# Expert products in plain float32: three groups of 32 slots in four column groups of TensorE, in place of split products over 128 slots

## The chip, the cores and the metric

One core of a Trainium2 chip runs the kernel. The metric is the device time of one launch in microseconds, lower is better. The core has a matrix engine (TensorE, PE in the rows; PEld is its weight load), three engines for elementwise work (VectorE or DVE, ScalarE or ACT, GpSimd or POOL), and SyncE (SP), which here starts nearly all DMA transfers. Sixteen DMA engines move the data between HBM and the on-chip memory. Products land in PSUM, eight banks of 128 partitions x 512 float32.

## What is computed

Two decoder layers over 256 tokens of width 1024. The change touches the last part of the second layer: eight experts, of which each token takes two.

```python
def swiglu(h, w_gate, w_up, w_down):
    return (jax.nn.silu(h @ w_gate) * (h @ w_up)) @ w_down

def moe_swiglu(h, w_router, w_gate, w_up, w_down):
    ...
    logits = (t @ w_router).astype(F32)
    top_v, top_i = lax.top_k(logits, TOP_K)
    wts = jax.nn.softmax(top_v, axis=-1)
    gate = jnp.sum(jax.nn.one_hot(top_i, N_EXPERTS, dtype=F32) * wts[..., None], axis=1)
    out = jnp.zeros((bsz * L, D), F32)
    for e in range(N_EXPERTS):
        ye = swiglu(t, w_gate[e], w_up[e], w_down[e]).astype(F32)
        out = out + gate[:, e:e + 1] * ye
```

D_MODEL is 1024, D_FF_EXPERT 3584, N_EXPERTS 8, TOP_K 2. All is float32: the experts' weights are 8 x 3 x 1024 x 3584 values, 352 MB, and each is read once.

## The kernel before

The kernel is written for each engine on its own, with semaphores between them. Both mixers and the dense channel mixer of layer one come first; `experts()` (one function for each engine, at L1290 for TensorE, L2004 for ScalarE, L2778 for VectorE) is the rest.

**Routing.** VectorE ranks the router's logits and gives each token a slot in each of its experts (`slot_of`). An expert has 128 slots. TensorE gathers the tokens of the first two experts by a product with a one-hot matrix (`gather`, L1481); for the others GpSimd fetches normalised rows from HBM by an indirect DMA (`taken`), and TensorE transposes them (`taken_transposes`, L1400). The outputs of experts 0 to 6 are scaled and added to rows in HBM by an indirect DMA of GpSimd (`sums`); those of expert 7 are combined on TensorE by another one-hot product.

**Split products.** A float32 product is made of three products of a rounded type (float32r). ScalarE rounds a weight tile to `hi` (L1910), VectorE subtracts to get `lo` (L2628), and `split_product` (L819 to L821) multiplies activation high by weight high, high by low and low by high. In each of them the activations are the stationary operand, 128 rows x 128 slots, and the weights are the moving one, 512 columns. `hi` and `lo` have three buffers each, so both engines run at most three tiles ahead of TensorE.

**Tiles and order.** A tile holds 2048 columns on 128 partitions, 1 MB: four blocks of 128 rows x 512 columns of a gate or up matrix, or 256 rows x 1024 of a down matrix. An expert takes 42 tiles in seven steps of 512 hidden columns: two gate, two up and two down tiles a step, with TensorE on the down tiles of one step behind the hidden ones of the next. Each tile costs TensorE 12 matmuls. SP loads them into a ring of seven places (`ring_e` and, for the seventh, `hT`); a place is free again when VectorE has made its `lo`. Between the steps ScalarE applies SiLU (L2074), VectorE multiplies (`act_product`, L2640), TensorE transposes the result (L1354) and both engines split it again (L2079, L2633).

**More than 128 tokens for one expert.** A second pass over all weights then runs; it is under an `If` on `most`, the largest count of tokens.

Of the kernel before, what the change touches and what calls it, by code (L numbers as in the profile page):

```python
# [20 lines left out]
P = 128  # L21
# [11 lines left out]
def decoder_trunk(nc, x_in, mem_in, positions, norm_mix, w_in, a_re, a_im, log_dt, b_re, b_im,  # L33
# [42 lines left out]
    MOE_TILES = 6 * NFE  # L76
    assert COLS == IN_FULL * BANK + 256 and FF % 256 == 0 and FE % BANK == 0 and NF % 2 == 1
# [13 lines left out]
    with ctx:  # L91
# [19 lines left out]
        normed = renamed("normed", [P, C, D], F32)  # L111
        xT_hi = sb("xT_hi", [P, KD, SEQ], F32R)
# [29 lines left out]
        memT = sb("memT", [P, KD, MEM])  # L142
        mask = sb("mask", [P, NG * 3 * P])
# [16 lines left out]
        last_ring.close()  # L160
        gT_hi = renamed("gT_hi", [P, KS, SEQ], F32R)
# [54 lines left out]
        fb = buffers(ffn)  # L216
        hi = fb("hi", [P, H, TILE], F32R)
# [20 lines left out]
        fb("idle", [P, (KD - 3) * P - 128])  # L238
# [3 lines left out]
        y_hi = fb("y_hi", [P, D], F32R)  # L242
        y_lo = fb("y_lo", [P, D], F32R)
# [11 lines left out]
        most = fb("most", [P, 1], I32)  # L255
        ffn.close()
# [13 lines left out]
        def combines_before(e):  # L270

            return e - (NE - 1)

# [167 lines left out]
        full_e = [sem(f"expert_tile_arrived_{r}") for r in range(RM)]  # L441
        params = sem("params_loaded")
        lrates = [sem(f"layer_rates_loaded{l}") for l in range(L)]
        lparams = [sem(f"layer_params_loaded{l}") for l in range(L)]
        N_SMALL = 7
        BASE = [0, MIX_TILES + FFN_TILES]

# [6 lines left out]
        def load_rates(queue, l):  # L454

            rates = lrates[l]
# [4 lines left out]
        def load_matrices(queue, l):  # L461

            s = lparams[l]
# [9 lines left out]
        def _(sp):  # L473
# [62 lines left out]
            def load_e(p, e, src, first):  # L536

                if not first or p >= RM:
                    sp.wait_ge(sem("lo_ready"), FFN_TILES + MOE_TILES * e + p - RM + 1)
                elif p == RM - 1:  # L540
                    sp.wait_ge(sem("logits_done"), 1)
                v = expert_tile(p).rearrange("p (k n) -> p k n", n=src.shape[2])
                sp.dma_start(v, src).then_inc(full_e[p % RM], 16)
# [12 lines left out]
            def expert_loads(e, turn, first):  # L556
                for i in range(4):
                    load_e(i, turn, moe_src(e, 0, i), first)
                for f in range(1, NFE):
                    for i in range(4):  # L560
                        load_e(6 * f - 2 + i, turn, moe_src(e, f, i), first)
                    for i in range(2):
                        load_e(6 * f + 2 + i, turn, moe_down_src(e, f - 1, i), first)
# [2439 lines left out]
```

## Time and profile before

| | |
|---|---|
| median of 3 runs | 1742.5 us (1740.66 to 1744.35) |
| span of the profiled execution | 1742.3 us |
| instructions in the profile | 22920 |
| TensorE busy in the span | 1719.4 us (99%) |
| VectorE busy | 1406.7 us (81%) |
| ScalarE busy | 1192.1 us (68%) |
| mean DMA rate | 280 GB/s |

The span runs from the first to the last instruction of the program; what lies around it is not more than the difference between span and median, 0.2 us. Busy time of TensorE counts an instruction from its start to its modelled end, and neighbours overlap: a matmul of 512 columns is listed with 0.39 us although the next one starts earlier. So its cost is read from the starts of a sequence, not from its duration. A plain float32 matmul has two records in the trace, a split product's matmul and a transpose one each.

### The profile page before, as it was taken

The numbers are of one execution on the slowest core, as the hardware profiler recorded it, in microseconds if no ns is written. First come the engines' busy times: TensorE is split into PE (matmuls) and PEld (weight loads), VectorE is DVE, ScalarE is ACT, GpSimd is POOL, SyncE is SP. The second block draws the span as 40 slices with busy tenths as digits, with TensorE's granted clock in tenths as the row PEclk, the third lists the DMA queues.
The fourth block names the chain that finished last, engine by engine and source line by source line (L and its number), as shares of the span: only waits on it lengthen the run. The fifth ranks groups of instructions, "written<-read, shape, count | busy, mean of one in ns | idle before, by whom it ended". The sixth has DMA issues, their size and how long they took to land.

```text
span 1742.3 us, 22920 instructions
## 1 busy us (share of the span) xinstructions
PE 1719.4 (99%) x8656; PEld 1422.1 (82%) x8656; DVE 1406.7 (81%) x1308; ACT 1192.1 (68%) x1405; POOL 166.0 (10%) x209
## 2 busy tenths in 40 slices
PE   9999999999999999999999999999999999999998
PEld 7778888888888888887888888888888888888886
DVE  8997557776658954768898888889888888888887
ACT  7877565744466755666777777777777777777775
POOL 5160000150001200010001010010000010000000
PEclk9999999999999999999999999999999999999999
DMA  7454436746545443489999999999999999999994
GB/s 243 143 165 138 133 121 202 226 161 203 169 146 169 146 145 121 154 312 359 378 347 410 368 372 393 379 376 384 364 393 379 360 401 372 372 392 376 380 400 167
DMA packets 224345, 488.62 MB, mean 280 GB/s; under 512 B 9660, under 2 KB 34360, under 8 KB 224248
## 3 DMA queue, kind: packets, MB, share of 16 engines
q1 hardware_dynamic: 220328, 474.07, 75.0%
q0 software_dynamic: 3824, 13.24, 2.8%
q8 instruction: 61, 1.00, 0.2%
q14 instruction: 36, 0.29, 0.0%
q10 hardware_dynamic: 96, 0.02, 0.0%
HBM read 479.43 MB, written 7.86 MB: 280 GB/s over the span
## 4 chain that ended last, share of the span: by engine, by line
PE 87%; DVE 9%; ACT 1%; issue 1%; DMA 0%; SPq 0%; DVEq 0%; ACTq 0%
PE ps L819 27%; PE ps L821 27%; PE ps L820 27%; DVE ring_lo L2190 3%; PE ps L1354 1%; PE ps L1096 1%; PE ps L812 1%; DVE turned L2448 1%; PE ps L1068 1%; DVE z L2406 1%; PE ps L1079 1%; ACT hi_m L1552 0%; DVE lo L2628 0%; DVE costab L2325 0%; DVE z L2391 0%
## 5 line engine op out<-in xcount | busy, mean ns | idle before, releaser
L2628 DVE TENSOR_TENSOR lo<-ring_e,hi 128x2048 fp32r<-128x2048 f32 x288 | 658.2, 2290 | 93.2 <-ACT hi L1910 91.3
L1910 ACT ACTIVATE hi<-ring_e 128x2048 fp32r<-128x2048 f32 x288 | 552.1, 1917 | 145.0 <-PE ps L821 144.4
L819 PE MATMUL ps<-hi,xe_hi 128*128 128x512 f32 x896 | 355.4, 397 | 4.4 <-DVE lo L2628 3.7
L821 PE MATMUL ps<-hi,xe_lo 128*128 128x512 f32 x896 | 350.4, 391 | 0.0
L820 PE MATMUL ps<-lo,xe_hi 128*128 128x512 f32 x896 | 350.0, 391 | 0.0
L1552 ACT ACTIVATE hi_m<-ring 128x1024 fp32r<-128x1024 f32 x160 | 160.6, 1054 | 116.0 <-PE ps L821 112.6
L2190 DVE TENSOR_TENSOR ring_lo<-ring,hi_m 128x1024 fp32r<-128x1024 f32 x160 | 190.0, 1229 | 33.4 <-ACT hi_m L1552 32.9
L821 PE MATMUL ps<-hi_m,xT_lo 128*128 128x512 f32 (+1 forms) x528 | 203.2, 385 | 0.0
L819 PEld LDWEIGHTS ps<-hi,xe_hi 128*128 128x128 f32 x896 | 168.8, 188 | 41.7 <-DVE lo L2628 4.1
L821 PEld LDWEIGHTS ps<-hi,xe_lo 128*128 128x128 f32 x896 | 168.7, 188 | 36.1
L820 PEld LDWEIGHTS ps<-lo,xe_hi 128*128 128x128 f32 x896 | 169.0, 189 | 33.3
L819 PE MATMUL ps<-hi,aT_hi 128*128 128x512 f32 x464 | 181.5, 391 | 0.1
L821 PE MATMUL ps<-hi,aT_lo 128*128 128x512 f32 x464 | 180.8, 390 | 0.0
L820 PE MATMUL ps<-lo,aT_hi 128*128 128x512 f32 x464 | 180.5, 389 | 0.0
L819 PE MATMUL ps<-hi_m,in_hi 128*128 128x512 f32 (+1 forms) x416 | 164.8, 396 | 4.9 <-DVE ring_lo L2190 3.6
L820 PE MATMUL ps<-ring_lo,in_hi 128*128 128x512 f32 (+1 forms) x416 | 159.4, 383 | 0.0
L2628 DVE TENSOR_TENSOR lo<-hT,hi 128x2048 fp32r<-128x2048 f32 x48 | 109.9, 2289 | 15.8 <-ACT hi L1910 15.4
L821 PEld LDWEIGHTS ps<-hi_m,xT_lo 128*128 128x128 f32 x528 | 99.5, 188 | 20.3
L1910 ACT ACTIVATE hi<-hT 128x2048 fp32r<-128x2048 f32 x48 | 92.0, 1916 | 25.8 <-PE ps L821 25.8
L819 PEld LDWEIGHTS ps<-hi,aT_hi 128*128 128x128 f32 x464 | 87.1, 188 | 18.3 <-issue 0.5
L821 PEld LDWEIGHTS ps<-hi,aT_lo 128*128 128x128 f32 x464 | 87.1, 188 | 18.3
L820 PEld LDWEIGHTS ps<-lo,aT_hi 128*128 128x128 f32 x464 | 87.2, 188 | 17.9
(446 smaller groups left out, 2417.0 us busy)
## 6 DMA issues: line engine op xcount, KB each, us to landing
ring_e<-in_moe_w_gate SPq DMA_DIRECT2D x104, 1024.0 KB, 7.6
ring_e<-in_moe_w_up SPq DMA_DIRECT2D x96, 1024.0 KB, 7.6
ring_e<-in_moe_w_down SPq DMA_DIRECT2D x88, 1024.0 KB, 7.3
ring<-in_w_in SPq DMA_DIRECT2D x50, 1024.0 KB, 5.0
hT<-in_moe_w_down SPq DMA_DIRECT2D x24, 1024.0 KB, 7.4
hT<-in_moe_w_up SPq DMA_DIRECT2D x16, 1024.0 KB, 7.0
ring<-in_ffn_w_gate SPq DMA_DIRECT2D x22, 512.0 KB, 3.9
ring<-in_ffn_w_up SPq DMA_DIRECT2D x22, 512.0 KB, 4.8
```

The source lines that it names most:

```text
L812: last = nc.tensor.transpose(o, a, ident[0:a.shape[0], 0:a.shape[0]])
L819: nc.tensor.matmul(o, x_hi, w_hi, start=first, stop=False, skip_group_check=True)
L820: nc.tensor.matmul(o, x_hi, w_lo, start=False, stop=False, skip_group_check=True)
L821: return nc.tensor.matmul(o, x_lo, w_hi, start=False, stop=end, skip_group_check=True)
L1068: last = nc.tensor.matmul(ps[:, bank, col:col + nk], qkT[o:o + HD, 0, hd // 2, c * P:(c + 1) * P], qkT[o:o + HD, 1, hd // 2, 0:nk], start= ...
L1079: nc.tensor.transpose(ps[:, 6 + b // 4, b % 4 * P:(b % 4 + 1) * P], pr[:, u % 2, b * P:(b + 1) * P], ident[:])
L1096: last = nc.tensor.matmul(ps[:, 5, o:o + v.shape[1]], pT[:, b * P:(b + 1) * P], v, start=first, stop=end, skip_group_check=True)
L1354: last = nc.tensor.transpose(ps[:, 2, j * P:(j + 1) * P], act_out[:, j * P:(j + 1) * P], ident[:])
L1552: nc.scalar.activation(hi_m[:, m % 2, o], ring[:, n % R, o], ACT.Copy).then_inc(sem("mixer_hi_ready"), 1)
L1910: nc.scalar.activation(hi[:, m % H, :], src, ACT.Copy).then_inc(sem("hi_ready"), 1)
L2190: V.tensor_tensor(ring_lo[:, n % R, o], ring[:, n % R, o], hi_m[:, m % 2, o].bitcast(F32), ALU.subtract).then_inc(sem("mixer_lo_ready"), 1)
L2628: last = V.tensor_tensor(lo[:, m % H, :], src, hi[:, m % H, :].bitcast(F32), ALU.subtract)
```

## The change

All products of the experts' first pass are plain float32, without `hi` and `lo`. An expert has 96 slots, three groups of 32. TensorE's 128 columns are used as four groups of 32: a matmul has 32 stationary columns and writes the 32 partitions of its group, and four of them stand in a row, one for each column group (a round).

- Gate and up: a tile is now one block of 128 rows x 1792 columns, half of an expert's hidden columns (896 KB). The four matmuls of a round take the same 32 slots as the stationary operand and four pieces of 448 columns as the moving one; all four results lie in one bank, that of the slots' group. Three rounds make a tile: 12 matmuls.
- Down: a tile is 256 rows x 1024 as before. Its 12 matmuls of 512 columns stand in three rounds (`DOWN_ROUNDS`), each with different stationary columns and with results in two banks. The third group of slots is summed in two places, which VectorE adds later.
- The hidden result (`acts`, slots on partitions) is made by VectorE in twelve operations of 32 partitions x 448 columns (`product`), which also bring the pieces from the partitions of the column groups to those of the slots. TensorE transposes it in 14 blocks a half.
- An expert is two halves. In half h TensorE does: gate (8 tiles), transposes of the second part of half h-1, three of its seven down tiles, up (8 tiles), the other four down tiles, transposes of the first part of half h.
- Loads: eight places for gate and up tiles (`ring_h`, `hT`), seven for down tiles (`ring_d`), in the order in which TensorE uses them. A place is free when TensorE has used it.
- VectorE scales an expert's rows (`expert_rows`), ScalarE no longer does.
- When an expert has over 96 tokens, two more passes of the old kind follow.
- The first pass is unrolled on all engines. The semaphores of the parameters' loads are shared between the layers.

The diff, cut to its core:

```diff
@@ -270,6 +284,22 @@
+        DOWN_ROUNDS = (((0, 0, 0), (0, 0, 1), (0, 0, 2), (0, 1, 1)),
+                       ((0, 1, 2), (1, 0, 1), (0, 1, 0), (1, 0, 2)),
+                       ((1, 0, 0), (1, 1, 2), (1, 1, 0), (1, 1, 1)))
...
@@ -533,14 +568,46 @@
+            def load_hidden(n, w, e, half, k):
+
+                if n >= RH:
+                    sp.wait_ge(sem("hidden_tiles_used"), n - RH + 1)
+                elif n == RH - 1:
                     sp.wait_ge(sem("logits_done"), 1)
+                src = w[0][e, k * P:(k + 1) * P, half * WIDE:(half + 1) * WIDE]
+                sp.dma_start(hidden_tile(k), src).then_inc(full_h[k], 16)
...
+            for t in range(HALVES):
+                for k in range(KD):
+                    load_hidden(2 * KD * t + k, moe_gate, t // 2, t % 2, k)
+                if t >= 2:
+                    load_downs(t - 1, 0)
+                for k in range(KD):
+                    load_hidden(2 * KD * t + KD + k, moe_up, t // 2, t % 2, k)
...
@@ -1381,50 +1446,176 @@
+                def columns_product(h, banks):
+
+                    e, own = h // 2, h // 2 % 2 * P
+                    for k in range(KD):
...
+                        pe.wait_ge(full_h[k], 16 * (n // RH + 1))
+                        w = hidden_tile(k)
+                        for g in range(3):
+                            for i in range(4):
+                                last = nc.tensor.matmul(ps[GROUP * i:GROUP * (i + 1), banks + g, 0:BLOCK],
+                                                        xe[:, k, own + GROUP * g:own + GROUP * (g + 1)],
+                                                        w[:, i * BLOCK:(i + 1) * BLOCK], start=k == 0, stop=k == KD - 1,
+                                                        skip_group_check=True)
+                        last.then_inc(sem("hidden_tiles_used"), 1)
...
+                def turned(h, part, bank=6, rows_of=None, slots_of=None):
+
+                    pe.wait_ge(sem("products_ready"), 2 * h + 1 + part if h > 0 else 2)
...
+                    for i in range(TURNED):
+                        t = TURNED * part + i
+                        o = ps[:, bank + i // 5, i % 5 * CAP:(i % 5 + 1) * CAP]
+                        last = nc.tensor.transpose(o, acts[0:CAP, t * P:(t + 1) * P], ident[0:CAP, 0:CAP])
...
+                        for round_ in DOWN_ROUNDS:
+                            for q, (odd, half, g) in enumerate(round_):
+                                only = g == 2
+                                last = nc.tensor.matmul(ps[GROUP * q:GROUP * (q + 1), 4 + half, :],
+                                                        aT[:, 2 * i + odd, GROUP * g:GROUP * (g + 1)],
+                                                        w[:, odd, half * BANK:(half + 1) * BANK],
...
+                        gate_columns(h)
...
+                        if h > 1:
+                            turned(h - 1, 1, rows_of=(rows_of, 1) if odd and rows_of else None,
+                                   slots_of=e // 2 + 1 if odd == 0 and e % 2 == 1 and e < NE - 1 else None)
+                            down_columns(h - 1, 0)
+                        up_columns(h)
...
+                        if h > 0:
+                            down_columns(h - 1, 1)
+                            turned(h, 0, rows_of=(rows_of, 2 if odd else 0) if rows_of else None)
...
@@ -2055,15 +2216,72 @@
+                    nc.scalar.activation(gates[:], ps[:, 0:3, 0:BLOCK], ACT.Silu).then_inc(sem("gates_ready"), 1)
...
@@ -2832,44 +3010,117 @@
+                def product(h):
+
+                    dve.wait_ge(sem("hidden_tiles_used"), 2 * KD * (h + 1))
+                    dve.wait_ge(sem("gates_ready"), h + 1)
+                    if h > 0:
+                        dve.wait_ge(sem("turned"), 2 * h)
+                    bank = 4 if h == 0 else 0
+                    for i in range(4):
+                        for g in range(3):
+                            last = V.tensor_tensor(acts[GROUP * g:GROUP * (g + 1), i * BLOCK:(i + 1) * BLOCK],
+                                                   ps[GROUP * i:GROUP * (i + 1), bank + g, 0:BLOCK],
+                                                   gates[GROUP * i:GROUP * (i + 1), g, :], ALU.mult)
...
+                def expert_rows(e):
+
+                    dve.wait_ge(sem("down_tiles_used"), 2 * DOWN_TILES * (e + 1))
+                    if e > 0:
+                        dve.wait_ge(sem("rows_added"), 16 * e)
...
```

On TensorE, in the middle of the first experts, hidden tiles and down tiles alternated before as split products; `hi`, `lo` are the weights' halves, `xe_hi` and `aT_hi` the activations':

```order
L819 MATMUL ps<-hi,xe_hi 128x512
L820 MATMUL ps<-lo,xe_hi 128x512
L821 MATMUL ps<-hi,xe_lo 128x512
L819 MATMUL ps<-hi,aT_hi 128x512 [waits lo_ready,actT_ready]
L820 MATMUL ps<-lo,aT_hi 128x512
L821 MATMUL ps<-hi,aT_lo 128x512
```

Now, at the end of a gate product, with the second part of `acts` turned and the first down tiles behind it (x11 is the rest of a tile's 12 matmuls):

```order
L1491 MATMUL ps<-hT,xe 32x448 [waits expert_tile_arrived_7]
L1491 MATMUL ps<-hT,xe 32x448 x11
L1523 MATMUL ps<-ident,acts 128x96 [waits slot_values_taken,aT_ready,products_ready]
L1523 MATMUL ps<-ident,acts 128x96 x6
L1455 MATMUL ps<-routes,disp 128x4 [waits dispatch_ready]
L1455 MATMUL ps<-routes,disp 128x4 x3
L1547 MATMUL ps<-ring_d,aT 32x512 [waits tile_arrived_0,aT_ready]
L1547 MATMUL ps<-ring_d,aT 32x512 x11
```

TensorE's waits for VectorE's `lo` are gone; it waits for the load of each tile itself, and for `products_ready` and `aT_ready` at the changes of stage.

On VectorE, between two steps of an expert before:

```order
L2628 TENSOR_TENSOR lo<-ring_e,hi 128x2048 [waits hi_ready]
L2640 TENSOR_TENSOR act_out<-ps,gate_act 128x512 [waits silu_done,split_used]
L2628 TENSOR_TENSOR lo<-ring_e,hi 128x2048 [waits hi_ready] x4
L2633 TENSOR_TENSOR aT_lo<-ps,aT_hi 128x512 [waits aT_hi_ready]
L2628 TENSOR_TENSOR lo<-ring_e,hi 128x2048 [waits hi_ready]
```

And now, over one `product` and the rows of an expert:

```order
L3022 TENSOR_TENSOR acts<-ps,gates 32x448 [waits turned,gates_ready,hidden_tiles_used]
L3022 TENSOR_TENSOR acts<-ps,gates 32x448 x11
L3038 COPY y_part<-ps 32x512 [waits rows_added,down_tiles_used]
L3039 TENSOR_TENSOR y_rows<-ps,y_part 32x512 [waits vector_chain]
L3041 COPY y_rows<-ps 64x512
L3038 COPY y_part<-ps 32x512
L3039 TENSOR_TENSOR y_rows<-ps,y_part 32x512 [waits vector_chain]
L3045 COPY y_rows<-ps 32x512 x2
L3050 TENSOR_SCALAR y_rows<-y_rows,slot_gate 96x1024 [waits slots_ready,y_taken]
```

The splits have left VectorE, and work on the results has come in their place.

## Rows read from the trace of the kernel before

**Rows 1.** Windows: busy time (and records) of each engine, clock, DMA share and rate.
```profile
core 0: us, PE busy (x) PEld busy (x) DVE busy (x) ACT busy (x) POOL busy (x), PEclk, DMA share, GB/s
776.00:1734.00 958.00, 953.51 (x4324) 786.76 (x4322) 843.32 (x496) 708.10 (x474) 42.38 (x38) 1.00 0.99 371
...
850.00:1700.00 850.00, 849.26 (x3866) 701.61 (x3865) 752.44 (x431) 635.22 (x421) 39.46 (x29) 1.00 1.02 380
```
**Rows 2.** Waits of TensorE in 776 to 1734 us: total, times, longest.
```profile
PE ps L819 <- DVE lo L2628: 3.7, 1, 3.7
```
**Rows 3.** Groups of VectorE and ScalarE, 776 to 1734: busy, mean ns, idle before.
```profile
L2628 DVE TENSOR_TENSOR lo<-ring_e,hi 128x2048 fp32r<-128x2048 f32 x286 | 653.6, 2290 | 93.1 <-ACT hi L1910 91.2
L2628 DVE TENSOR_TENSOR lo<-hT,hi 128x2048 fp32r<-128x2048 f32 x48 | 109.9, 2289 | 15.8 <-ACT hi L1910 15.4
...
L1910 ACT ACTIVATE hi<-ring_e 128x2048 fp32r<-128x2048 f32 x286 | 548.2, 1917 | 142.0 <-PE ps L821 141.4
```
**Rows 4.** Timeline of TensorE at 1000 us: start, duration, what.
```profile
999.74 0.39 PE L821 MATMUL ps<-hi,xe_lo 128*128 128x512 f32 x1
...
1002.01 0.60 PE L1354 MATMUL ps<-ident,act_out 128*128 128x128 f32 x4
1002.44 1.04 PE L1400 MATMUL ps<-ident,taken 128*128 128x128 f32 x8
1003.24 0.48 PE L819 MATMUL ps<-hi,xe_hi 128*128 128x512 f32 x1
```
**Rows 5.** Timeline at 119 us, and L1002's records: ns minimum, median, maximum.
```profile
119.88 1.08 PE L1002 MATMUL ps<-z,cT 128*32 128x128 f32 x32
120.89 0.50 PE L819 MATMUL ps<-hi_m,in_hi 128*128 128x512 f32 x1
...
L1002 PE MATMUL ps<-z,cT x256: 269/273/297, 91.8 to 588.5; 128*32 128x128 f32 x128
```
**Rows 6.** Records of a plain float32 product over the whole array, 256 columns.
```profile
L1059 PE MATMUL ps<-kmT,qmT x32: 379/379/435, 213.2 to 697.7; 128*128 128x256 f32 x32
```
**Rows 7.** Timeline of TensorE at 59 us, and L957's records.
```profile
59.13 0.39 PE L821 MATMUL ps<-hi_m,xT_lo 128*128 128x512 f32 x1
59.45 0.86 PE L957 MATMUL ps<-cT,z 128*32 128x32 f32 x64
60.23 0.50 PE L819 MATMUL ps<-hi_m,in_hi 128*128 128x512 f32 x1
60.57 0.39 PE L820 MATMUL ps<-ring_lo,in_hi 128*128 128x512 f32 x1
...
L957 PE MATMUL ps<-cT,z x64: 196/196/217, 59.4 to 60.1; 128*32 128x32 f32 x64
```
**Rows 8.** Operations of 512 columns from PSUM on VectorE and ScalarE.
```profile
L2640 DVE TENSOR_TENSOR act_out<-ps,gate_act x56: 676/683/692, 793.8 to 1724.1; 128x512 f32<-128x512 f32 x56
...
L2074 ACT ACTIVATE gate_act<-ps x56: 582/587/602, 782.5 to 1719.4; 128x512 f32<-128x512 f32 x56
```
**Rows 9.** Timeline of the stage's first matmul and of its end.
```profile
776.17 0.47 PE L819 MATMUL ps<-hi,xe_hi 128*128 128x512 f32 x1
...
1733.56 0.39 PE L821 MATMUL ps<-hi,aT_last 128*128 128x512 f32 x1
1733.99 0.60 ACT L2124 ACTIVATE y_hi<-ps 128x512 fp32r<-128x512 f32 x1 [0.68 <-PE ps L821]
...
1735.22 2.71 DVE L2831 SCALAR_TENSOR_TENSOR x<-ps,gate,x 128x512 f32<-128x512 f32 x4
```
**Rows 10.** The page's rate in 40 slices, and loads: KB each, us to landing.
```profile
GB/s 243 143 165 138 133 121 202 226 161 203 169 146 169 146 145 121 154 312 359 378 347 410 368 372 393 379 376 384 364 393 379 360 401 372 372 392 376 380 400 167
...
ring_e<-in_moe_w_gate SPq DMA_DIRECT2D x104, 1024.0 KB, 7.6
...
ring_e<-in_moe_w_down SPq DMA_DIRECT2D x88, 1024.0 KB, 7.3
ring<-in_w_in SPq DMA_DIRECT2D x50, 1024.0 KB, 5.0
```

More of the change, by code:

```diff
@@ L1390, in slot_rows, with taken_transposes @@
                     last.then_inc(sem("slot_values_done"), 1)
[L1392 removed]
+                def taken_transposes(e, part):
                     pe.wait_ge(sem("rows_taken"), 16 * (e - 1))
[L1395 to L1401 removed]
@@ new lines, in first_pass @@
+                def first_pass():
+                    dispatch(0)
+                    normed_rows_low(1)
+                    busiest_expert()
+                    for half in range(2):
+                        scale_gathered(0, half, 6 - 2 * half)
+                    route_weights()
+                    dve.wait_ge(sem("gain_row_loaded"), 16)
+                    for c in range(C):
+                        last = V.scalar_tensor_tensor(out=normed[:, c, :], in0=x[:, c, :], scalar=rs[:, 2 + c:3 + c],
+                                                      in1=gain_row[:], op0=ALU.mult, op1=ALU.mult)
+                    last.then_inc(sem("rows_normed"), 1)
+                    ramps_of_last()
+                    for h in range(HALVES):
+                        e, odd = h // 2, h % 2
+                        if odd == 0 and e % 2 == 1 and e < NE - 1:
+                            dve.wait_ge(sem("slot_values_done"), e // 2 + 1)
+                            dispatch(e + 1)
+                        if h == HALVES - 2:
+                            last_dispatch()
+                        product(h)
+                        if odd == 0 and e > 0:
+                            expert_rows(e - 1)
+                    last_rows()
@@ L2953, in one_pass @@
-                    expert(NE - 2, NE // 2 - 1 + pair0, 0, False, False, not base)
+                    for i in range(3):
+                        split(i, base)
+                    for half in range(2):
+                        scale_gathered(pair0, half, 6 - 2 * half)
+                        gathered_low(base, 0, half)
+                    expert(0, pair0, 0, True, False)
+                    expert(1, pair0, 1, False, False)
+                    with dve.Fori(1, NE // 2 - 1) as p:
+                        expert(2 * p, p + pair0, 0, False, False)
+                        expert(2 * p + 1, p + pair0, 1, False, False)
```

610 lines of the change are left out of this document (346 added, 264 removed).

## Prediction, made before the changed kernel was run

> **What bounds the kernel now.** I read the windows first [rows 1]. The expert layer lasts from 776 to 1734 us: 958 of 1742.3 us of span. TensorE is busy in 953.5 of them, VectorE in 843, ScalarE in 708; the granted clock is 1.00, which is the 2.4 GHz level. The waits then say who is late: in all of the stage TensorE waited once for VectorE, 3.7 us [rows 2], while ScalarE stood 141.4 us for TensorE to give back a split buffer [rows 3]. So TensorE sets the stage, and splitting (653.6 + 109.9 us on VectorE, about as much on ScalarE) is hidden work that is worth nothing when it goes. The sixteen DMA engines stand beside TensorE with a share of 1.02 at 380 GB/s [rows 1], yet no wait names them. Whether they have room is the open question.
>
> **The stage today, as a check of the method.** 336 tiles with 12 matmuls each are 4032. Ten of them start between 999.74 and 1002.01, so one costs 0.227 us [rows 4]: 915 us. Twelve transposes start between 1002.01 and 1003.24, 0.10 us each [rows 4]; there are 272: 27 us. That makes 942 of 958; the rest, 16 us, is the 3.7 us wait and some 0.03 us at each of 336 tiles (semaphores, the restart after transposes).
>
> **What a round costs after the change.** The trace already has plain float32 in column groups: L1002 (128 rows x 32 columns stationary, 128 moving columns, four groups that write one bank). Each such matmul has two records. 32 records, that is eight rounds of four, lie in 1.08 us, and the median record takes 0.273 us [rows 5]; seven steps fill 1.08 - 0.27 us, so a round costs at most 0.116 us. The clock's own price comes from the record's length against its columns: 273 ns at 128 and 379 ns at 256 columns [rows 5, 6], 0.83 ns a column, two cycles at 2.4 GHz, or 0.106 us a round. So four groups run side by side, the weight loads hide, and a round adds 0 to 0.010 us to its stream. I take 0.005.
> - Gate and up tile: three groups of 32 slots, two rounds each, 448 columns: 6 x (0.371 + 0.005) = 2.26 us. 16 halves x 16 = 256 tiles: 578 us.
> - Down tile: three rounds of four, twice, 512 columns: 6 x (0.424 + 0.005) = 2.57 us. 112 tiles: 288 us.
> - Sum 866 us, with ends 855 and 877, against 915. Ninety-six slots instead of 128 and four float32 passes instead of three split products just cancel (3/4 x 4 = 3); what is gained is the 0.014 us that a split matmul needs above its 512 columns (0.227 against 0.213), which column rounds don't show.
>
> **What else lies on TensorE's path.** Transposes: 14 per half of `acts` make 224, and 48 of `taken`, all with 96 moving columns; the row has 0.10 us for 128, so 27 us at most, 22 if they shrink. Change of array shape: around the column blocks, 59.13 to 59.45 and 60.23 to 60.57 cost 0.32 and 0.34 us where 0.227 is normal, and L1002's 1.01 us to the next start holds 0.87 us of rounds [rows 4, 5, 7], so there and back is 0.3 to 0.4 us. Each half has two blocks of transposes: 32 x 0.34 = 11 us, ends 7 and 13. Semaphores: 368 tiles x 0.03 = 11 us, ends 0 and 18. Stage: 866 + 27 + 11 + 11 = 915 us.
>
> **What is taken off without effect, and its cover.** The splits go. `product` puts twelve 32 x 448 operations on VectorE; a 512-column one takes 0.683 us [rows 8], so at most 12 x 0.68 = 8.2 us. The next gate product waits for all twelve; in between TensorE has four down tiles and seven transposes, 10.3 + 0.7 us. If that cover failed by 1 us, it would cost 16. The SiLU of 1344 columns, 0.587 us for 512 [rows 8] and so below 1.8 us, lies under three down tiles (7.7 us), and with it the copies that bring the transposed blocks back. `expert_rows` comes once an expert, eight operations, under 7 us by the same row; TensorE needs its `y_taken` only after eight gate tiles, 18 us, and the scatter that its `rows_added` wait is for was started a whole expert earlier. Behind it on VectorE stands only the next `product`, two products of TensorE away. SP's loads stand in the order of use; a blocked up tile holds back down tiles behind it, but TensorE then still has 11 to 15 tiles ahead (8 places and 7).
>
> **Ends.** The gather ends and the first expert matmul starts at 776.17 [rows 9]; after the change the gate product needs `xe` scaled, in two operations of 1024 columns, each below 1.4 us by the same row; the first runs beside the gather's second half and the second is needed only at the fifth tile: 776.3. The end: today half of the last output is split before the down product ends, 1733.56 to 1735.22 from last product to first addition [rows 9]. Now the first half needs copy 0.60, subtraction 0.68 [rows 8] and two matmuls after the last product: +1.1 us, and 0.4 us for four more transposes. Today 1742.3 - 1734 = 8.3 us follow; then 9.8.
> 776.3 + 915 + 9.8 = 1701 us of span. The median of 1742.5 is 0.2 us over the span, so it stands for it. By the ends of the terms: 855+22+7+0 gives 1670, 877+27+13+18 gives 1721; the terms are independent, and 1690 to 1712 holds most of it.
>
> **Rivals.**
> *A, the DMA engines set the pace.* The stage moves 958 x 371 GB/s = 355 MB [rows 1]. In 915 us that is 388 GB/s. Against room: the share is 1.02 over 850 us at 380 GB/s, and a tile lands in 7.6 us where the mixer's needs 5.0 [rows 10], so it queues. For room: slices of 43.6 us reach 410 and 401 GB/s with the same 2 KB rows [rows 10], the rows become 7 KB, and 4 KB rows land in 7.3 us. If 380 is the ceiling: 355/0.380 = 934 us, 776 + 934 + 12 = 1722. Between 380 and 388: 1702 to 1722. A ceiling of 360, the lowest full slice, would be 986 us and 1774; it is level with today at 373.
>
> *B, the weight loads don't hide, and it is slower.* The mechanism is the load of 32 columns that each record needs: 2208 rounds of four. L957 has streams of only 32 columns (0.027 us a round), so loads bind there: 64 records, 16 rounds, in 0.86 us of which 0.20 is the last record [rows 7], 0.044 us a round. Were that added to each stream, 2208 x (0.044 - 0.005) = 86 us more: 1787. It turns to a loss when a round costs over 0.024 us above its stream. L1002 speaks against: 0.106 + 0.044 = 0.150 us, and a round takes 0.116 at most [rows 5]. But its rounds are short and its run is 1 us; 448 columns from four places of a tile, for 18 us, with the DMA engines full, are not in the trace, nor are down rounds that write two banks.
> The Trainium skill, TensorE: Matmul & The Clock Gate, "What overlaps and what doesn't", says that weight loads overlap running matmuls only where the row group differs; here all four groups share their rows, so by that rule B would hold. The trace disagrees, at 128 columns. The same page's table has three column groups at 2.38 times one instead of 3; by that efficiency 855 us of streams would be 1078 and the kernel 1913, an estimate from that page, which L1002 does not bear out either.
>
> *C, more than 96 slots.* The third pass and its fellow run when an expert has over 96 tokens; then two more passes of the old kind follow, some 1900 us. From the reference's inputs I counted the tokens of each expert: 91, 59, 77, 54, 60, 52, 66, 53. Five spare, so this stays out.
>
> *D, no change.* The 41 us come back through stalls of 2.5 us a half: `product` late (the cover of 11 us against 8.2), `turned` held by `xe_taken`, or the shape change dearer in long streams. It would give 1740.
>
> **How the numbers follow.** Forecast 1701: 0.50. A: 0.27, of which 0.03 is beyond 1739. B: 0.12. C: 0.01. D and partial forms of it: 0.10, half of it within the bound of no change and half below. A measurement of this kernel tells 0.2%, 3.5 us, from no change. Faster: 0.50 + 0.24 + 0.05 = 0.79; the same 0.05; slower 0.16 (B, C and the tail of A). The range takes in the forecast's terms and A to a partial D: 1688 to 1744; below it I leave 0.05, above it 0.15.
>
> **What the profile after would show.** Starts of gate or up tiles 2.25 to 2.30 us apart, of a down tile 2.57 to 2.60; PE idle of less than 1 us before L1491 with `products_ready`; twelve `acts` operations in under 8.2 us; splitting gone from the experts and VectorE under 300 us busy there; 385 to 392 GB/s at share 1.0. If A holds, L1491 and L1547 wait for DMA, tiles land in 8 us or more and the rate stays at 380. If B holds, there are no waits and a gate tile takes 2.5 us. I would be wrong in the method if one round of 448 columns took over 0.40 us without any wait before it.

## The result, and the profile after

The changed kernel takes 1687.45 us (median; 1685.9 to 1687.7), the kernel before 1743.2 us in the same comparison: ratio 0.9677, interval 0.9663 to 0.9690, 56 us less. The forecast was 1701, 42 us less, with a range from 1688. The direction and the mechanism held; the time is 13.5 us under the forecast and 0.5 us under the range.

The profiled execution has a span of 1685.7 us. Windows of it (us; busy us and records of each engine; granted clock; DMA share; GB/s), to set beside [rows 1], then the waits of TensorE from 776 us to the end (total, times, longest), beside [rows 2]; the one at L1575 lies behind the stage:

```profile
776.00:1676.00 900.00, 898.84 (x9124) 309.52 (x9121) 166.45 (x278) 51.32 (x104) 22.10 (x36) 1.00 0.99 394
850.00:1650.00 800.00, 800.00 (x8114) 274.84 (x8110) 150.48 (x247) 43.94 (x91) 19.89 (x29) 1.00 1.01 401
```
```profile
PE ps L1575 <- DVE y_lo L3077: 1.6, 1, 1.6
PE ps L1523 <- ACT slot_values L2251: 1.2, 1, 1.2
```

The stage went from 958 to 900 us. TensorE is still what sets it: in 850 to 1650 us it is busy for all of the 800. VectorE fell from 843 to 166 us and ScalarE from 708 to 51; all that this gave by itself is that the one stall behind VectorE [rows 2] is gone. No wait of TensorE names a DMA, though the rate rose from 371 to 394 GB/s. The timeline of TensorE (start, duration, what) from one gate product to the next; x168 is seven tiles, x24 one:

```profile
870.09 15.99 PE L1491 MATMUL ps<-ring_h,xe 128*32 128x448 f32 x168
885.90 2.44 PE L1491 MATMUL ps<-hT,xe 128*32 128x448 f32 x24
888.27 0.80 PE L1523 MATMUL ps<-ident,acts 96*128 96x96 f32 x7
888.84 0.59 PE L1455 MATMUL ps<-routes,disp 128*128 128x4 f32 x4
889.36 7.93 PE L1547 MATMUL ps<-ring_d,aT 128*32 128x512 f32 x72
897.11 15.97 PE L1491 MATMUL ps<-ring_h,xe 128*32 128x448 f32 x168
912.89 2.44 PE L1491 MATMUL ps<-hT,xe 128*32 128x448 f32 x24
915.15 10.48 PE L1547 MATMUL ps<-ring_d,aT 128*32 128x512 f32 x96
925.56 0.80 PE L1523 MATMUL ps<-ident,acts 96*128 96x96 f32 x7
```

A product of eight tiles that follows a down block, 897.11 to 915.15, takes 18.04 us: 2.255 a tile, and 0.3758 for each of its 48 round steps, against a stream of 448 columns x 0.8333 ns = 0.3733. A round costs 2.5 ns above its stream, and nothing is left over for a tile. The one that follows transposes, 870.09 to 888.27, takes 18.18, 0.14 us more. Three down tiles take 7.75 us (889.36 to 897.11), 2.58 each. VectorE's and ScalarE's own work there, by groups (busy, mean ns, idle before), and the loads (KB each, us to landing; beside [rows 8] and [rows 10]):

```profile
L3022 DVE TENSOR_TENSOR acts<-ps,gates 32x448 f32<-32x448 f32 x192 | 119.0, 620 | 690.8 <-PE ps L1491 688.2
L2226 ACT ACTIVATE gates<-ps 128x1344 f32<-128x1344 f32 x16 | 20.7, 1291 | 274.3 <-PE ps L1491 274.3
```
```profile
GB/s 248 151 151 149 126 125 175 219 213 186 176 131 171 172 133 142 126 250 294 423 423 416 413 408 394 422 387 398 405 419 386 386 394 422 405 381 398 420 387 146
...
ring_d<-in_moe_w_down SPq DMA_DIRECT2D x112, 1024.0 KB, 14.0
ring_h<-in_moe_w_gate SPq DMA_DIRECT2D x112, 896.0 KB, 9.7
```

Twelve operations on `acts` are 12 x 0.620 = 7.4 us, below the 8.2 allowed and the cover of 11. The loads take 10 and 14 us to land, longer than before, yet TensorE waits for none of them: they are issued earlier than they are needed. The end, beside [rows 9]:

```profile
1676.21 1.08 ACT L2263 ACTIVATE y_hi<-ps 128x512 fp32r<-128x512 f32 x2 [17.30 <-PE ps L1547]
...
1677.68 0.47 PE L1575 MATMUL ps<-y_hi,last_dispT 128*128 128x512 f32 x1 [1.60 <-DVE y_lo L3077]
...
1678.52 2.73 DVE L3009 SCALAR_TENSOR_TENSOR x<-ps,gate,x 128x512 f32<-128x512 f32 x4 [0.39 <-PE ps L1576]
```

### The profile page after: what moved, and what is told of

It is laid out like the page before. It is cut to its first block, busy times and chain, and to the rows that moved or that the text cites. A ratio compares the mean times of both kernels' runs of the same rounds, so it can differ in the third digit from the quotient of the medians.

```text
span 1685.7 us, 30528 instructions
## 1 busy us (share of the span) xinstructions
PE 1664.6 (99%) x13458; PEld 945.5 (56%) x13458; DVE 726.5 (43%) x1090; ACT 530.5 (31%) x1031; POOL 144.5 (9%) x209
## 4 chain that ended last, share of the span: by engine, by line
PE 88%; DVE 9%; issue 1%; ACT 1%; DMA 0%; DVEq 0%; ACTq 0%
PE ps L1491 34%; PE ps L1547 17%; PE ps L884 10%; PE ps L886 9%; PE ps L885 9%; DVE ring_lo L2389 3%; PE ps L1523 1%; PE ps L1161 1%; PE ps L877 1%; DVE turned L2647 1%; PE ps L1133 1%; DVE z L2605 1%; PE ps L1144 1%; ACT hi_m L1728 0%; DVE costab L2524 0%
## 5 line engine op out<-in xcount | busy, mean ns | idle before, releaser
L1491 PE MATMUL ps<-ring_h,xe 128*32 128x448 f32 x5376 | 511.4, 539 | 0.0
L3022 DVE TENSOR_TENSOR acts<-ps,gates 32x448 f32<-32x448 f32 x192 | 119.0, 620 | 690.8 <-PE ps L1491 688.2
L1491 PEld LDWEIGHTS ps<-ring_h,xe 128*32 128x32 f32 x5376 | 173.1, 110 | 325.9 <-issue 324.0
L1547 PE MATMUL ps<-ring_d,aT 128*32 128x512 f32 x2688 | 294.2, 593 | 0.0
L1547 PEld LDWEIGHTS ps<-ring_d,aT 128*32 128x32 f32 x2688 | 85.8, 110 | 191.9 <-issue 190.5
L884 PEld LDWEIGHTS ps<-hi_m,in_hi 128*128 128x128 f32 x416 | 78.2, 188 | 25.9 <-issue 4.3
L2827 DVE TENSOR_TENSOR lo<-ring,hi 128x2048 fp32r<-128x2048 f32 x33 | 75.8, 2306 | 27.0 <-ACT hi L2086 27.0
L885 PEld LDWEIGHTS ps<-ring_lo,in_hi 128*128 128x128 f32 x416 | 78.3, 188 | 13.9
L1491 PE MATMUL ps<-hT,xe 128*32 128x448 f32 x768 | 78.0, 539 | 0.0
L884 PE MATMUL ps<-hi_m,xT_hi 128*128 128x512 f32 x176 | 69.6, 395 | 2.3 <-DVE ring_lo L2389 1.5
```

The lines of the kernel that those rows point to most:

```text
L884: nc.tensor.matmul(o, x_hi, w_hi, start=first, stop=False, skip_group_check=True)
L885: nc.tensor.matmul(o, x_hi, w_lo, start=False, stop=False, skip_group_check=True)
L1491: last = nc.tensor.matmul(ps[GROUP * i:GROUP * (i + 1), banks + g, 0:BLOCK], xe[:, k, own + GROUP * g:own + GROUP * (g + 1)], w[:, i * BLO ...
L1547: last = nc.tensor.matmul(ps[GROUP * q:GROUP * (q + 1), 4 + half, :], aT[:, 2 * i + odd, GROUP * g:GROUP * (g + 1)], w[:, odd, half * BANK ...
L2827: last = V.tensor_tensor(lo[:, m % H, :], src, hi[:, m % H, :].bitcast(F32), ALU.subtract)
L3022: last = V.tensor_tensor(acts[GROUP * g:GROUP * (g + 1), i * BLOCK:(i + 1) * BLOCK], ps[GROUP * i:GROUP * (i + 1), bank + g, 0:BLOCK], gat ...
```

## Experiments

All ratios are against the kernel before, measured beside the experiment; a difference from the changed kernel is against 1687.45 us.

**1. Price of a change of shape.**
```diff
                         w = hidden_tile(k)
+                        if k > 0:
+                            nc.tensor.transpose(ps[:, 3, 0:CAP], ident[0:CAP, :], ident[0:CAP, 0:CAP])
```


> The changed kernel with one transpose of 96 columns (over the whole array) ahead of the gate and up tiles k = 1 to 7 of every product, 224 more; they write a bank that nothing reads. Theory of the prediction: there and back costs 0.34 us and the transpose 0.08, 224 x 0.42 = 94 us, so 1781. From the trace of the changed kernel I expect less: it shows 0.2 to 0.3 us there and back around a block of transposes, 224 x (0.08 + 0.25) = 74 us, 1761. If a change of shape cost nothing of its own: 18 us, 1705.

Measured: 1771.45 us, ratio 1.016 (1.0143 to 1.0177), 84.0 us more, 0.375 us each. The timeline of TensorE:
```profile
1003.71 2.46 PE L1493 MATMUL ps<-ring_h,xe 128*32 128x448 f32 x24
1006.10 0.30 PE L1490 MATMUL ps<-ident 96*128 96x96 f32 x1
1006.33 2.46 PE L1493 MATMUL ps<-ring_h,xe 128*32 128x448 f32 x24
```
From tile to tile it is 2.62 us where 2.255 is normal: 0.365, and less the transpose itself (0.083 us, the distance of two starts inside a block) there and back is 0.28 to 0.29 us. The forecast's 0.34 was 0.05 us too much; that a change costs nothing is excluded. I had expected 74 us from the blocks of the changed kernel, which I had read a little too low.

**2. Price of a satisfied wait.**
```diff
                         for g in range(3):
+                            pe.wait_ge(full_h[k], 16 * (n // RH + 1))
                             for i in range(4):
...
                         for round_ in DOWN_ROUNDS:
+                            pe.wait_ge(full_d[n % RD], 16 * (EARLIER[n % RD] + n // RD + 1))
```


> The changed kernel with the wait on the arrived tile repeated ahead of every round of a tile (satisfied already), 736 more on TensorE. The prediction's term of 0.03 us for each semaphore gives 736 x 0.03 = 22 us, 1709. If a satisfied wait costs TensorE nothing while rounds are queued, 1687.5 as before, and gate tiles still start 2.255 us apart.

Measured: 1686.26 us, ratio 0.967 (0.9654 to 0.9686): 1.2 us less than the changed kernel, so no difference. A product after transposes still takes 18.18 us (870.00 to 888.18):
```profile
870.00 15.99 PE L1492 MATMUL ps<-ring_h,xe 128*32 128x448 f32 x168
...
888.18 0.80 PE L1524 MATMUL ps<-ident,acts 96*128 96x96 f32 x7
```
The expectation called this 736 more waits; the edit repeats the wait ahead of every round, the first one too, so it is 3 x 368 = 1104. At 0.03 us each they would cost 33 us. They cost nothing: the term of 11 us for semaphores is gone.

**3. A fourth round.** In each gate and up tile, with the first group of slots once more.
```diff
-                        for g in range(3):
+                        for g in range(4):
...
-                                                        xe[:, k, own + GROUP * g:own + GROUP * (g + 1)],
+                                                        xe[:, k, own + GROUP * (g % 3):own + GROUP * (g % 3 + 1)],
```


> The changed kernel with a fourth round in each gate and up tile (the first 32 slots again, into a bank that nothing reads), as 128 slots would need in gate and up alone. By the price of a round, 0.376 us twice in 256 tiles: 256 x 0.752 = 192.5 us more, 1880, slower than the kernel before. If part of the stage were set by the DMA engines, it would be less than that: a stage that DMA bounds in half of its tiles would give about 1780.

Measured: 1879.24 us, ratio 1.0777 (1.0755 to 1.0798), 191.8 us more for 512 round steps: 0.3746 each. Rounds are the whole of what a tile costs; with room for 128 slots the scheme would be a loss. The windows of this run are worth a look for the DMA share:
```profile
850.00:1800.00 950.00, 950.00 (x9709) 325.73 (x9707) 146.48 (x240) 42.67 (x90) 20.09 (x30) 1.00 0.93 332
```
At 332 GB/s the share is still 0.93.

**4. Where the DMA engines end.** Two groups of slots in place of three.
```diff
-                        for g in range(3):
+                        for g in range(2):
...
-        DOWN_ROUNDS = (((0, 0, 0), (0, 0, 1), (0, 0, 2), (0, 1, 1)), ...
+        DOWN_ROUNDS = (((0, 0, 0), (0, 0, 1), (0, 1, 0), (0, 1, 1)),
+                       ((1, 0, 0), (1, 0, 1), (1, 1, 0), (1, 1, 1)))
```


> The changed kernel with two groups of slots in place of three; the third group's products are left out, so the rows of slots 64 to 95 are not computed. TensorE needs 256 x 1.504 + 112 x 1.716 + 34 = 611 us instead of 900, so the DMA engines must set the stage, and its 355 MB in its time is their ceiling. Rival A with 380 GB/s gives 934 us, 1720; with the 394 GB/s of the changed kernel as the ceiling 900 us, 1687, no change; I expect 415 GB/s, as its best slices had (up to 423), 855 us and 1641.

Measured: 1647.37 us, ratio 0.9447 (0.9428 to 0.9466). Windows, and the first waits of TensorE:
```profile
850.00:1600.00 750.00, 589.66 (x5320) 161.40 (x5324) 138.20 (x224) 43.92 (x91) 19.84 (x29) 0.99 1.02 415
```
```profile
PE ps L1546 <- DMA ring_d<-in_moe_w_down: 57.3, 90, 2.7
PE ps L1490 <- DMA ring_h<-in_moe_w_gate: 56.6, 78, 3.5
PE ps L1490 <- DMA ring_h<-in_moe_w_up: 54.4, 103, 2.4
```
Now TensorE waits for loads, 179 us in all, and the rate stays at 415 GB/s. That is the ceiling for these loads, and rival A's 380 was none. The changed kernel at 394 has 5% of room; below some 1645 us nothing on TensorE would pay. The share was 1.02 at 380 GB/s before the change, is 1.02 at 415 here, and 0.93 at 332 in experiment 3: it tells that transfers are in flight, not that they can't go faster.
The Trainium skill, DMA: Bandwidth & Descriptors, "Where 436 GB/s comes from", has about 358 GB/s for each core, half of what an HBM stack gives to two, as what binds loads from HBM, and 435 as the ceiling of the fabric. This run, with one core alone, moved 415 GB/s, above the first and below the second.

**5. The order inside a tile.**
```diff
-                        for g in range(3):
-                            for i in range(4):
+                        for i in range(4):
+                            for g in range(3):
```


> The changed kernel with the two inner loops of a gate or up tile exchanged: three matmuls in a row go to the same 32 columns of the array, then three to the next. If TensorE starts matmuls in order and each waits for its own column group, only the ones at the border of two groups run side by side: eight streams of 0.376 us twice over instead of six steps... taken for a tile of twelve matmuls, 8 x 0.376 = 3.0 us for each record's stream counted once, with two records a matmul up to 4.5 to 6.0 us; so at least 256 x 0.75 = 192 us more, 1880, and up to 256 x 3.7, 2640. If each column group had a queue of its own, nothing changes: 1687.

Measured: 1954.67 us, ratio 1.1212 (1.1188 to 1.1236), 267 us more, 1.04 us a tile. The wording of the expectation is muddled; its two ends for matmuls that start in order are 1880 and 2640, and the time lies near the lower. A tile is 3.3 us. A block of TensorE's timeline with the change from its seventh tile (`ring_h`) to the eighth (`hT`), and weight loads:
```profile
1049.21 22.42 PE L1491 MATMUL ps<-ring_h,xe 128*32 128x448 f32 x164
1071.10 0.56 PE L1491 MATMUL ps<-hT,xe 128*32 128x448 f32 x1
1071.43 0.57 PE L1491 MATMUL ps<-ring_h,xe 128*32 128x448 f32 x2
...
1071.84 0.54 PE L1491 MATMUL ps<-ring_h,xe 128*32 128x448 f32 x1
...
1072.22 0.54 PE L1491 MATMUL ps<-ring_h,xe 128*32 128x448 f32 x1
```
```profile
1015.29 0.17 PEld L1491 LDWEIGHTS ps<-ring_h,xe 128*32 128x32 f32 x4 [0.24 <-issue]
1015.69 0.14 PEld L1491 LDWEIGHTS ps<-ring_h,xe 128*32 128x32 f32 x2 [0.24 <-issue]
1016.07 0.17 PEld L1491 LDWEIGHTS ps<-ring_h,xe 128*32 128x32 f32 x4 [0.23 <-issue]
```
Six loads every 0.78 us, 0.13 us a record, where the changed kernel has four every 0.376, 0.094 a record. So it isn't one matmul after another, and it isn't four at a time: about three run side by side. A column group does not have an endless queue of its own. The first record of the eighth tile starts at 1071.10, with four records of the seventh still to start, at 1071.43 (two), 1071.84 and 1072.22: the start of a record does run ahead, but only by a few. The starts fit this reading: the six records of a column group are 0.376 us apart, and the next group begins behind the third of them, every 0.782 us. A product of eight tiles is then 32 x 0.782 us and 1.5 us for the end of the last group, 26.5 us; from 1049.21 to the transposes at 1075.81 it took 26.6. Why the look-ahead ends there is open. The rounds are needed: without them gate and up take nearly half as long again (3.3 us a tile against 2.255).

**6. Same stationary columns and one bank.** The rounds mix groups of slots and banks.
```diff
-                        for g in range(3):
-                            for i in range(4):
+                        for turn in range(3):
+                            for i, g in enumerate(((0, 1, 2, 0), (1, 2, 0, 1), (2, 0, 1, 2))[turn]):
```


> The changed kernel with rounds of four in which the column groups hold different stationary columns (slots groups 0, 1, 2, 0, then 1, 2, 0, 1, then 2, 0, 1, 2) and write three banks in place of one. Theory: only the four different column groups matter, since the down rounds, with two banks and mixed columns, show 0.429 us against a stream of 0.427; so 1687.5 as before. Rival, that a round needs its one stationary and its one bank: a split of each round in two, 1536 x 0.19 = 290 us more, or a few ns a round, 1536 x 0.005 = 8 us.

Measured: 1686.37 us, ratio 0.9678 (0.966 to 0.9695): no difference from the changed kernel. The last tile of a product takes 2.37 us up to the transposes, as in the changed kernel (885.90 to 888.27):
```profile
885.04 2.44 PE L1491 MATMUL ps<-hT,xe 128*32 128x448 f32 x24
887.41 0.80 PE L1523 MATMUL ps<-ident,acts 96*128 96x96 f32 x7
```
Four different column groups are all that a round needs. That its matmuls share their stationary columns and their bank, as the change has it, plays no part in the time.

**7. Fewer slots without column groups.** The kernel before with 96 stationary columns.
```diff
-    last = split_product(ps[:, bank, :], xe_hi[:, kk, :], xe_lo[:, kk, :], w_hi[:, k, :],
+    last = split_product(ps[0:96, bank, :], xe_hi[:, kk, 0:96], xe_lo[:, kk, 0:96], w_hi[:, k, :],
```
and the same in `down`.


> The kernel before with 96 stationary columns in place of 128 in all split products of the experts (slots 96 to 127 hold no tokens, and are left out). Theory: a split matmul of 512 moving columns costs 0.227 us whatever its stationary width, so 1743, no change; the fewer slots pay only in column groups. Rival: the 0.014 us above the stream is the load of 128 columns, and shrinks with it to 0.010, 4032 x 0.0035 = 14 us less, 1729.

Measured: 1752.97 us, ratio 1.0055 (1.0037 to 1.0073): 10 us slower. Neither theory had that. Starts of TensorE behind the same stall as before:
```profile
786.76 0.47 PE L819 MATMUL ps<-hi,xe_hi 128*96 128x512 f32 x1 [3.64 <-DVE lo L2628]
787.07 0.39 PE L820 MATMUL ps<-lo,xe_hi 128*96 128x512 f32 x1
...
789.38 0.40 PE L821 MATMUL ps<-hi,xe_lo 128*96 128x512 f32 x1
```
Ten steps take 2.31 us. Over 850 to 1700 us the mean step is 0.2300 us against 0.2273 before; 4032 x 0.0027 = 11 us. The 14 ns above the stream (0.2273 against 512 columns at 2.4 GHz, 0.2133) don't shrink with the load, they grow by 3. Why is open. The slots alone are worth less than nothing; they pay only with the column groups.

**8. The stall at 784 us.** In the kernel before, VectorE's order at the start of the stage.
```diff
                         for half in range(2):
                             first_odd(half)
-                        busiest_expert()
-                        route_weights()
-                        dve.wait_ge(sem("gain_row_loaded"), 16)
-                        for c in range(C):
-                            last = V.scalar_tensor_tensor(out=normed[:, c, :], in0=x[:, c, :], ...
-                        last.then_inc(sem("rows_normed"), 1)
...
                     split(3, e)
...
+                    if scattered and first_one:
+                        busiest_expert()
+                        route_weights()
                     for i in range(4, 6):
                         split(i, e)
+                    if scattered and first_one:
+                        dve.wait_ge(sem("gain_row_loaded"), 16)
+                        for c in range(C):
+                            last = V.scalar_tensor_tensor(out=normed[:, c, :], in0=x[:, c, :], ...
+                        last.then_inc(sem("rows_normed"), 1)
                     act_product(a0 + 1, M + s0 + 4)
```


> The kernel before with one edit of order on VectorE: the routing weights stand behind the fourth split, and the two operations on normed behind the sixth, instead of ahead of them. Theory: the stall of 3.7 us at 784 goes but for 0.7 us, and with it the 11 matmuls at 0.427 us (2.3 us): 5.3 us less, 1738. It is a part of the 16 us that the prediction had spread over 336 tiles. If those 16 us lay with the tiles, only the stall would go, 3 us, and TensorE's clock fall would stay. If VectorE were late elsewhere for it, no change.

Measured: 1738.66 us, ratio 0.9978 (0.9967 to 0.9989), 4.5 us less. From its first expert matmul (774.59) to the first of the last output (1728.28) are 953.7 us, where before has 776.17 to 1734.18, 958.0. First the stall in before, the steps behind it, and the window of 788 to 793 us, where the granted clock is 0.50, the 1.2 GHz level:
```profile
788.36 0.80 PE L819 MATMUL ps<-hi,xe_hi 128*128 128x512 f32 x1 [3.69 <-DVE lo L2628]
788.96 0.63 PE L820 MATMUL ps<-lo,xe_hi 128*128 128x512 f32 x1
789.38 0.63 PE L821 MATMUL ps<-hi,xe_lo 128*128 128x512 f32 x1
...
788.00:793.00 5.00, 4.64 (x11) 3.67 (x12) 4.71 (x3) 0.00 (x0) 0.00 (x0) 0.50 1.00 324
```
Then the waits of this run and the same place in it:
```profile
PE ps L819 <- DVE lo L2628: 1.6, 2, 1.2
```
```profile
786.68 0.47 PE L819 MATMUL ps<-hi,xe_hi 128*128 128x512 f32 x1 [0.37 <-DVE lo L2628]
786.99 0.40 PE L820 MATMUL ps<-lo,xe_hi 128*128 128x512 f32 x1
```
The stall shrank by 2.1 us, and the steps of 0.427 us behind it, which cost before some 2.3 us, are not there. So part of the residual that the prediction spread over all tiles sat in one place. Experiment 7 adds a limit: there TensorE waited 3.64 us at the same point and went on at 0.23 us a step, with a granted clock of 1.00 from 784 to 794 us, so a stall of this length does not always bring the clock down. It seems to do so mostly. Of the ten runs of before that stand beside this experiment, nine have a mean granted clock of 0.994 or 0.995 and take 1742.3 to 1744.4 us, and one has 0.998 and 1739.9; of the four runs of experiment 7 three have 0.995 and some 1753 us, and the profiled one 0.997 and 1750.15; here seven of eight have 0.997 or 0.998. So the fall is most likely in the median of before. A mean clock doesn't tell where it fell, so this is argued, not shown.

**9. Plain float32 without column groups.** Gate and up as four matmuls a tile over the whole array.
```diff
-                        for g in range(3):
-                            for i in range(4):
-                                last = nc.tensor.matmul(ps[GROUP * i:GROUP * (i + 1), banks + g, 0:BLOCK],
-                                                        xe[:, k, own + GROUP * g:own + GROUP * (g + 1)],
+                        for i in range(4):
+                            last = nc.tensor.matmul(ps[0:CAP, banks + i, 0:BLOCK], xe[:, k, own:own + CAP],
```


> The changed kernel with plain float32 but no column groups in gate and up: four matmuls a tile over the whole array (128 rows, 96 stationary columns, 448 moving columns) into four banks, in place of twelve in column groups; the results lie where the next stage doesn't look, so they are not used. One part of the change alone. A matmul is two records of 448 columns at 0.83 ns, 0.373 us each, eight steps a tile where the rounds have six. Were a record's price above its stream the 2.5 ns of the rounds: 3.006 us a tile, 256 x 0.751 = 192 us more, 1880. Were it the 14 ns of the split products: 3.098 us, 216 us more, 1903. If the second is measured, the gain above the stream comes from the column groups, if the first, from plain float32.

Measured: 1879.3 us, ratio 1.0781 (1.0749 to 1.0812), 191.9 us more: the 2.5 ns theory to the microsecond. Timeline of one stretch:
```profile
999.50 12.94 PE L1490 MATMUL ps<-ring_h,xe 128*96 128x448 f32 x34
```
34 records: 33 steps in 12.94 - 0.54 us (the last record's length), 0.3758 each, the step of a round. This gives two results. A round of four column groups costs what a single matmul over the array, here with 96 stationary columns, costs; one group alone could not be done before its own 448 columns, 0.3733 us, so a round does nearly four times the work of one. And the low price above the stream comes with plain float32, not with the groups.
The Trainium skill, TensorE: Matmul & The Clock Gate, gives three column groups as 2.38 times one ("Measured speedup vs the span model") and weight loads as overlapping running matmuls only where row groups differ ("What overlaps and what doesn't"). Both measurements speak against it: a round of four on the same rows steps by 0.3758 us with four loads of 0.110 us in it, and a single matmul by the same 0.3758 with one of 0.163 us, where the stream alone is 0.3733.

**10. What a split product pays above its stream.** The kernel before with 384 moving columns in gate and up.
```diff
-    last = split_product(ps[:, bank, :], xe_hi[:, kk, :], xe_lo[:, kk, :], w_hi[:, k, :],
-                         w_lo[:, k, :], kk == 0, kk == KD - 1)
+    last = split_product(ps[:, bank, 0:384], xe_hi[:, kk, :], xe_lo[:, kk, :], w_hi[:, k, 0:384],
+                         w_lo[:, k, 0:384], kk == 0, kk == KD - 1)
```


> The kernel before with 384 moving columns in place of 512 in every gate and up matmul of the experts; the other 128 columns of each tile are left out. 384 columns take 0.160 us at 2.4 GHz. Theories for the 14 ns that a split matmul shows above its 512 columns: a fixed price gives steps of 0.174 us, a proportional one 0.170 us, and a bound by the weight load, whose records last 0.188 us, steps of 0.188 us or more. TensorE's part of the stage falls by 2688 x 0.053 = 143, 153 or 105 us; the DMA ceiling of 415 GB/s (855 us for 355 MB) and the 843 us of VectorE don't let the whole of it through: 1640 to 1665 in all cases, so the step is to be read in the trace, in a tile that waits for nothing.

Measured: 1673.69 us, ratio 0.9601 (0.9573 to 0.9629). The step in a tile that waits for nothing, and the load that goes with it:
```profile
1000.52 0.34 PE L821 MATMUL ps<-hi,xe_lo 128*128 128x384 f32 x1
...
1002.09 0.34 PE L821 MATMUL ps<-hi,xe_lo 128*128 128x384 f32 x1
```
```profile
PE ps L819 <- DVE lo L2628: 41.6, 62, 4.8
```
```profile
L820 PEld LDWEIGHTS ps<-lo,xe_hi 128*128 128x128 f32 x760 | 143.9, 189 | 1.2
```
Nine steps in 1.57 us, 0.174 each; the most frequent single step is 0.173. Above the stream of 0.160 that is 13 to 14.4 ns, and with 512 columns it is 14.0: the price is fixed. A price in proportion to the columns would be 10.5. The load's record, 0.189 us, is longer than the step and does not bind: records overlap, so their length is not a price. The time is 9 us above the range that I gave: VectorE's splits now hold TensorE up, 41.6 us in 62 waits, with the DMA engines at 407 GB/s.

Nor does the price come from what runs beside TensorE. In the kernel before, over the last products of the stage, VectorE, ScalarE, GpSimd and the DMA engines stand still:
```profile
1731.00:1732.60 1.60, 1.60 (x9) 1.33 (x8) 0.00 (x0) 0.00 (x0) 0.00 (x0) 1.00 0.00 0
```
```profile
1731.07 0.39 PE L819 MATMUL ps<-hi,aT_last 128*128 128x512 f32 x1
...
1732.43 0.39 PE L819 MATMUL ps<-hi,aT_last 128*128 128x512 f32 x1
```
Six steps in 1.36 us, 0.227 each, as in the middle of the stage. What it is in a split matmul that costs the 14 ns stays open.

## Why the prediction was right, and where it was wrong

**The bound and the rounds.** TensorE was named as the bound and is. Rounds were put at 866 us; 1536 steps of 0.3759 and 672 of 0.429 are 865.7. Inside it two small errors cancel: the stream is 0.8333 ns a column, not 0.83 (860 us, not 855), and a round adds 2.5 ns, not 5.

**Where the 58 us of the stage came from.** Before, 4032 split matmuls x 0.2273 = 916.4 us; after, 865.7: 50.7 us, of the same 3/4 x 4 = 3 passes. The fixed 14 ns of each split matmul are 4032 x 0.0140 = 56 us, the 2.5 ns of each round 5.5 us; that difference, 51 us, is the gain. Experiments 9, 10 and 7 show its parts: it is plain float32 that lacks the 14 ns, column groups are what makes plain float32 payable, and the 96 slots what makes it three rounds. The other 7 us: the stall behind VectorE and the slow clock after it (6.2 us) went, of which the prediction had only the wait of 3.7 us as a piece of its own, the transposes became 2.7 us cheaper, and small things took 1.6 back.

**The step that failed: the last 16 us of the old stage, spread over its tiles.** "Some 0.03 us at each of 336 tiles" was the remainder of a sum, and nothing in the trace showed it. It was carried over as 368 x 0.03 = 11 us. Experiment 2 shows the price of a satisfied wait as nil, and a run of eight tiles in 18.04 us leaves nothing for one. In before the 16 us are: the stall 3.7 and the slow steps behind it 2.5; 66 first products, behind transposes or at the start of an expert, at 0.09 (0.31 us to the next start where 0.227 is normal), 5.8; seven borders between experts at 0.27, 1.9; 16 small products on `routes`, 1.8; loose ends. None of it grows with tiles. And one part was counted twice: the prediction named "the restart after transposes" as part of the 0.03 us, and then put 11 us for the changes of shape, which hold the same restarts, beside it.

**The sizes that were off.** From 775.88 to 1676.0 us there are 900.1 us for a forecast of 915:
- transposes 272 x 0.0825 = 22.4, forecast 27; the lower end that the prediction named was right: inside a block transposes start 0.108 us apart with 128 moving columns before, and 0.0825 with 96 now;
- changes of shape 8.2, forecast 11: 0.29 us there and back by experiment 1, for some 30 blocks;
- semaphores 0, forecast 11; but 3.8 us are left over, of which the timeline shows some 3.2 in 16 small products on `routes`, the wait of 1.2 us for `slot_values` and four late transposes, which the sum had not named;
- rounds 0.3 below.
Together 14.9. The start came 0.4 us earlier, the tail was 9.7 for 9.8. The median stands 1.75 us above the profiled span, where 0.2 had been read for the kernel before: 0.4 + 14.9 + 0.1 - 1.8 = 13.6, the miss. The 0.2 set the median of some runs beside the span of another; every run of either kernel lies some 1.7 us above its own core's span (1687.46 and 1685.7 here, 1744.08 and 1742.4 before).

**The range.** By the ends of its terms the sum could be 1670, and 1690 was made of that because the terms were taken as independent. They were not: restarts stood both in the semaphore term and in the changes of shape, and transposes, changes and semaphores all missed to the same side. A time below 1688 had been given a chance of 0.05.

**The rivals.** A (DMA engines at 380 GB/s) fell: 394 in the stage without a wait for a load, 415 as the ceiling (experiment 4). The row for it was there, two slices over 400 in [rows 10], and the share of 1.02 that spoke for it is no measure of a ceiling. (The lowest full slice there reads 347 GB/s, not 360; it was no ceiling either.) B (loads not hidden) fell: 2.5 ns a round. C did not come up. D did not either: the cover of `product` held, 7.4 us under 11, and the stall at `slot_values` came once, for the first pair.

## What to carry to other kernels

Count columns x passes / groups side by side, and then look at the fixed price of each instruction: here three split passes of 128 slots and four plain ones of 96 stream the same, and 14 ns a matmul decided. Split products in column groups would by the same count be 3 x 3/4 = 2.25 passes; no run here tried them. Fill all four column groups by consecutive matmuls; what they hold and which bank they write does not matter. Do not carry the remainder of a sum over to a new kernel as so much for each tile: find it in the timeline first, it may be one stall.

## What was not expected of the hardware

- A split matmul (fp32r) costs 14.0 ns above its stream with 512 moving and 128 stationary columns, 13 to 14.4 with 384 moving columns, and 16.7 with 96 stationary columns: narrower was slower. Plain float32 costs 2.5 ns a record over the whole array and a round of four column groups.
- With consecutive matmuls on one column group about three of four groups still run side by side (0.13 us a record against 0.094), and a record starts ahead of up to four that stand before it.
- The DMA share stands at 0.93 at 332 GB/s, at 1.01 at 401 and at 1.02 at 380 and 415.
- A stall of 3.7 us on TensorE was followed by 11 steps of 0.427 us and more at a granted clock of 0.50 in one execution, and one of 3.64 us by none, at 1.00, in another.
